# Closing an attention unit ahead of the exponentials, and a rearranged first pair of tiles, in a transformer step on 8 cores

## The reference, cut to what matters

```python
def layer(x, mod):                        # same weights for context and latent tokens
    x += 0.5*gate1 * SwiGLU(RMSNorm(x)*(1+scale1)+shift1)      # FFN 1, 1024 -> 2x2816 -> 1024
    h  = RMSNorm(x)*(1+scale2)+shift2
    dq, dk, dv, gq, gk, gv = split(h @ w_in)                   # 1024 -> 2304
    # 4 differential heads: softmax(q1 k1) - lam*softmax(q2 k2), times v, then RMSNorm of the head
    # 8 grouped query heads on 2 kv heads
    x += gate2 * (concat(o_diff, o_gqa) @ w_out)
    x += 0.5*gate3 * SwiGLU(RMSNorm(x)*(1+scale3)+shift3)      # FFN 2
mod = silu(c) @ w_ada + b_ada             # 9 vectors of 1024: shift, scale, gate, three times
```

## Time and profile before

| | |
|---|---|
| median of 3 runs | 3947.0 us |
| profiled execution | 3947.68 us; span of its slowest core (core 3) 3946.2 us |
| spans of the 8 cores | 3928.2 to 3946.2 us |
| granted TensorE clock, mean | 0.959 to 0.963 |
| busy: PE, DVE, ACT, POOL | 89%, 59%, 52%, 3% |
| DMA | 572.79 MB, 145 GB/s on average |

### The profile page before, as it was taken

How to read it: one execution, slowest core, us unless ns; L and a number is a source line. 1 busy time by engine, 2 the same in 40 slices (tenths; PEclk the granted TensorE clock), 3 DMA queues, 4 the chain that set the end, 5 groups by cost and what they waited for, 6 DMA issues and landing times.

```text
span 3946.2 us, 51478 instructions; the slowest of 8 cores (3928.2 to 3946.2 us)
## 1 busy us (share of the span) xinstructions
PE 3505.6 (89%) x15812; PEld 1523.4 (39%) x15812; DVE 2322.3 (59%) x3013; ACT 2048.4 (52%) x2608; POOL 99.9 (3%) x183
## 2 busy tenths in 40 slices
PE   1996899998869698998999999899989999899988
PEld 0442344443334344444334444333423433334433
DVE  5665774543554755565755676655567655655643
ACT  2213323334443434443576766677776667777631
POOL 0000000001010000000000000000000000000000
PEclk9998899999989799999999999999999999999989
DMA  8787776666536267565523423422233313332232
GB/s 215 174 208 203 210 259 186 197 210 168 166 110 187 77 179 213 176 206 198 165 88 112 136 81 115 152 92 79 90 115 133 106 63 105 133 104 86 89 124 95
DMA packets 134842, 572.79 MB, mean 145 GB/s; under 512 B 16848, under 2 KB 22480, under 8 KB 129744
## 3 DMA queue, kind: packets, MB, share of 16 engines
q1 hardware_dynamic: 118304, 491.56, 37.6%
q0 software_dynamic: 16272, 77.93, 9.2%
HBM read 540.40 MB, written 90.51 MB: 160 GB/s over the span
## 4 chain that ended last, share of the span: by engine, by line
PE 65%; ACT 15%; DVE 9%; issue 6%; DMA 4%; ACTq 0%; DVEq 0%; SPq 0%; POOL 0%; POOLq 0%
PE PSA L464 65%; ACT PT L467 10%; ACT L467 2%; DVE RG L470 1%; DVE MT L473 1%; DVE XB L473 1%; ACT HB L467 1%; DVE FIN L477 1%; DVE FIN L484 1%; DMA DR<-w_dn 1%; DVE PT L473 1%; DMA PT<-w_ada 1%; DVE NS L470 1%; ACT FIN L467 1%; DMA s_vd<-RG 1%
## 5 line engine op out<-in xcount | busy, mean ns | idle before, releaser
L464 PE MATMUL PSA<-HB,WR 128*128 128x512 bf16 x6800 | 1577.4, 388 | 143.1 <-ACT HB L467 58.4
L467 ACT ACTIVATE PT<-PSA 128x1024 bf16<-128x1024 f32 x1184 | 1151.5, 1021 | 344.3 <-PE PSA L464 324.0
L464 PEld LDWEIGHTS PSA<-HB,WR 128*128 128x128 bf16 x6800 | 669.9, 99 | 1025.9 <-issue 290.4
L464 PE MATMUL PSA<-QTS,RG 128*128 128x512 bf16 (+1 forms) x2432 | 659.4, 375 | 74.5 <-ACT PT L467 70.8
L464 PE MATMUL PSA<-PT,RG 128*128 128x512 bf16 (+1 forms) x2368 | 648.4, 381 | 28.8 <-DVE FIN L477 22.8
L464 PE MATMUL PSA<-HID,DR 128*128 128x512 bf16 x2640 | 590.8, 380 | 17.3 <-DMA DR<-w_dn 13.9
L467 ACT ACTIVATE TH<-PSA 128x512 f32<-128x512 f32 x352 | 209.6, 596 | 576.5 <-PE PSA L464 566.9
L473 DVE SCALAR_TENSOR_TENSOR TH<-TH,PSA 128x512 f32<-128x512 f32 x352 | 241.3, 686 | 343.4 <-ACT TH L467 339.6
L464 PEld LDWEIGHTS PSA<-HID,DR 128*128 128x128 bf16 x2640 | 258.0, 98 | 333.5 <-issue 26.1
L464 PEld LDWEIGHTS PSA<-QTS,RG 128*128 128x128 bf16 (+1 forms) x2432 | 195.1, 97 | 467.8 <-issue 333.6
L467 ACT ACTIVATE SQ<-XB 128x512 f32<-128x512 f32 x224 | 139.5, 627 | 431.0 <-DVE XB L473 392.6
(11 more groups left out here) (89 smaller groups left out, 1655.9 us busy)
## 6 DMA issues: line engine op xcount, KB each, us to landing
WR<-s_gu SPq DMA_DIRECT2D x308, 512.0 KB, 4.1
DR<-s_dn SPq DMA_DIRECT2D x112, 704.0 KB, 4.6
RG<-s_kt SPq DMA_DIRECT2D x64, 576.0 KB, 4.1
WR<-s_in SPq DMA_DIRECT2D x65, 512.0 KB, 5.6
RG<-s_vg SPq DMA_DIRECT2D x32, 864.0 KB, 6.4
PT<-w_ada SPq DMA_DIRECT2D x48, 512.0 KB, 8.2
RG<-s_vd SPq DMA_DIRECT2D x32, 576.0 KB, 4.8
XB<-xs SPq DMA_DIRECT2D x8, 2048.0 KB, 9.9
```

The source lines that it names most:

```text
L464: return ("pe", (lambda e: e.matmul(out, lhsT, rhs, start=start, stop=stop)), reads, [PK(bank)], c, None, mode)
L467: return ("act", (lambda e: e.activation(out, in_, func, **kw)), reads, writes, 0.18 + n * 0.00082, None)
```

## The change

Four things are changed. (1) `fin_d` and `fin_g` are spawned with priority 2 and so rank above exponentials, additions and everything else where the planner finds no difference in idle time. (2) For the pair of tiles, the squares are summed by TensorE: `stats_pe` sends each of the eight squares through an fp32 matmul with ones into one bank, and the additions on DVE and the matmul in `norm` fall away. (3) The cast loads of FFN 1 weight blocks 2 and later wait for shift 1 (`MOD 0`) instead of scale 1 (`MOD 1`), and so do the write-backs of blocks 0 to 5; the second tile's x is loaded after 15 pieces of `w_ada` instead of 9. (4) The Silu of c comes right after c's load, and the lambda computation waits until shift 1 is done.

```diff
+            early = kind == "gu0" and idx < NW
+
             def wb():
-                yield [dma("sp", s_w[kind][idx], dst, [key], [("sw", kind, idx)], nsem("wb", 4), nb // 2)]
+                if early:
+                    yield Get(ev(("mod", 0)))
+                yield [dma("sp", s_w[kind][idx], dst, [key] + ([("MOD", 0)] if early else []), [("sw", kind, idx)], nsem("wb", 4), nb // 2)]
                 setf(("wb", kind, idx))
-            gate = [("MOD", 1)] if kind == "gu0" else [("HID", 10)] if kind == "dn0" else []
+            gate = [("MOD", 1) if idx < 2 else ("MOD", 0)] if kind == "gu0" else [("HID", 10)] if kind == "dn0" else []
...
-                    yield Get(ev(("mod", 1)))
+                    yield Get(ev(("mod", 1 if i < 2 else 0)))
...
+        yield [act(CB.rearrange("p g d -> p (g d)"), CB.rearrange("p g d -> p (g d)"), AF.Silu, ["FIN"], ["FIN"], n=2048)]
+        setf("CB")
         yield [dma("sp", BADA[:, :], b_ada[:, :], [], ["BADA"], "c1", 36864)]
...
-        yield [act(CB.rearrange("p g d -> p (g d)"), CB.rearrange("p g d -> p (g d)"), AF.Silu, ["FIN"], ["FIN"], n=2048)]
-        setf("CB")
+        yield Get(ev(("mod", 0)))
...
-                if (m, c) in ((1, 3), (0, 1)):
+                if (m, c) in ((1, 3), (0, 7)):
                     put("xgo")
...
+    def stats_pe(xb):
+
         b = yield Get("bank")
-        yield [mm(PSB[b], ONESF[:, :], NS[:, xb, :], [("NS", xb), "ONESF"], b, cost=0.9)]
+        for c in range(8):
+            s = yield Get("SQ")
+            yield [act(SQ[:, s, :], XB[:, xb, c, :], AF.Square, [("X", xb, c)], [("SQ", s)])]
+            yield [mm(PSB[b], ONESF[:, :], SQ[:, s, :], [("SQ", s), "ONESF"], b, start=(c == 0), stop=(c == 7), cost=0.9)]
+            put("SQ", s)
+        put(("stp", xb), b)
...
-            stats(xb, None, prio)
+            S.spawn(stats_pe(xb), prio)
...
-            yield from norm(xb, 0, 1, h)
+            yield from norm(xb, 0, 1, h, True)
...
-                S.spawn(fin_d(q, u, ot) if kind == "d" else fin_g(q, u, ot), A_PRIO)
+                S.spawn(fin_d(q, u, ot) if kind == "d" else fin_g(q, u, ot), 2)
```

More of the change, by code:

```diff
@@ L645, in stats, with norm @@
         S.spawn(run(), prio)
-    def norm(xb, i, g, h):
-        yield Get(("st", xb))
-        yield Get("NORM")
+    def stats_pe(xb):
         b = yield Get("bank")
-        yield [mm(PSB[b], ONESF[:, :], NS[:, xb, :], [("NS", xb), "ONESF"], b, cost=0.9)]
+        for c in range(8):
[4 more added lines that the diff above has]
+        put(("stp", xb), b)
+    def norm(xb, i, g, h, pe=False):
+        if pe:
+            b = yield Get(("stp", xb))
+            yield Get("NORM")
+        else:
+            yield Get(("st", xb))
+            yield Get("NORM")
+            b = yield Get("bank")
+            yield [mm(PSB[b], ONESF[:, :], NS[:, xb, :], [("NS", xb), "ONESF"], b, cost=0.9)]
         for o in rstd_ops(b, 1.0 / D, RSTD[:, :], ["RSTD"]):
```

## The result

The changed kernel took 3881.63 us (median of 4 runs, 3880.25 to 3888.57), the kernel before 3947.01 in the same session. The ratio is 0.984, with a 95% interval of 0.982 to 0.986: 65 us less, 1.6%. The prediction was 3872 us, with a range from 3840 to 3910.

The account below looks back on a forecast made before the run. The change was taken to pay only where TensorE, the busiest engine, has nothing to do. Attention -42, end -15 and start -19 sum to -76 on 3947.7 us, giving 3872 us, range 3840 to 3910.

Parts of the forecast that it names:

- the end: After the last PV matmuls: HB 8.5 us earlier and a projection of 19 us instead of 25, together -15 us.
- Halts: Attention: fifteen stretches without exponentials, where units wait for closings stuck behind exponentials, vanish, -85 us.
- Pace of keys without filler: Attention: with filler running out earlier, ACT-paced keys lose 17 us less, DVE-paced keys in differential units 4 us more.
- Filled closings: Attention: at 12 of 16 closings, with filler around, ACT has 17.6 us against TensorE's 15.4, +2 each, +24 us.
- Recip and copies without filler: Attention, differential units without filler: grouped closing's copies, reciprocal and product add to DVE's work, 5 us in each of six, +30.
- (b): Attention keys without filler where ACT sets the pace, 0.09 us lost a key; claimed to fall by 17 us.
- more: Rival: the attention's new costs hide behind exponentials running ahead, attention -66, total 3848 us; chance 0.20.
- The start: Before the first HB matmul: shift 1 ready at 63 us instead of 87.6, first HB matmul sooner, -19 us.
- Eaten by the queue: Rival: each closing holds the exponentials 2 us longer, the attention gives only -12, total 3902 us; chance 0.13.
- Switches cost more: Rival: table switches between exponentials in the attention cost another 1.3 us each, total 3903 us; chance 0.05.
- Start gives nothing: Rival: held-back casts leave FFN 1 short of weights and take the 19 us back, total 3891 us; chance 0.07.
- Slower: Rival: a differential closing's chain of about 11 us blocks ACT and holds the exponentials, +100, 4047 us; chance 0.05.

Follow-up runs that it names:

- the start's own run: The changed kernel with both closings put back at the rank of the exponentials, leaving the start's edits alone: 0.9958 of the kernel before, -17 us.

## Why the prediction was right where it was

**The time** is 10 us off the point forecast, within the range, and the forecast case is the one that came: halts gone, filler running out earlier, switches paid for, start and end shorter.

**The step that failed** is in "the end": "HB is there near 3765.5, 8.5 earlier", added to the attention's -42. The attention's window reaches to that very chunk, and the 44 matmuls beside the closing are in its 7478 records. They cost 9.5 us wherever they stand, so the -42 had the gain in it already. The run with only the last closing first shows it: 13.2 of 15.7 us given back. Without the 8.5 the recorded terms give -42 - 6.5 - 19 = -67.5. That they then sum to exactly the span's change is partly luck, as the terms show.

**The attention's terms**, from the loss record by record and the runs:

- Halts, -85: the first 12 keys of differential units lost 119 us before and lose 39 now, -80. That has in it the 15 that grouped closings now add there (below), so the halts gave some 95, ten more than recorded.
- Pace of keys without filler, -17 and +4: the keys 12 to 36 of grouped units lost 37 and, without the 13 of the next item, lose 32, so about -5, not -17; the same keys of differential units lost 27 and lose 39, +12, not +4. The first was too large by some 10, the second too small by 8.
- Filled closings, +24: 13, shown by the kernel without switches. The 17.6 us on ACT against 15.4 named the place and nearly the price, 1.5 to 1.9 us for 2; but such closings are eight, not twelve.
- Recip and copies without filler, +30: those four stretches lose 15 more than the pace of additions; the reciprocal alone is 13 by its own run. The term was twice what came, since four stretches paid, not six, and less than 5 us each.
- Not foreseen: +14 at the beginning of grouped units, where TensorE waits for ACT, most of it in the four ahead of which filler had run out.
- Together: -95 - 5 + 12 + 13 + 15 + 14 = -46, where 189.4 became 144.5. That the recorded terms came to -42 all the same is luck in their errors: the gain of the halts too small, two costs and the gain of (b) too large, the +4 too small, and +14 left out. (These counts end with the last exponential; up to HB it is the -42.5 of the table.)
- The bounds don't follow from the terms: with all new costs hidden these give -103, not -85, and with half as much again and nothing from (b) they give +5.5. The -66 of "more" hides the +24 alone.

**The end**: 24.1 us from the last PV matmuls to the projection's sum, predicted 27. The projection's own part was 16.3, not 19, since TensorE took its 64 matmuls after a pause of 5.68 us at nearly its full pace.

**The start**: -16.2 on the slowest core, predicted -19. (By the recorded terms, squares from 58 and 16.4 us for eight at the low clock give 74.4, not 73.5.) Shift 1 came at 70.1, not 63, the squares at 65.7, not 58, the first HB matmul at 75.6, not 70: the second x was sent at 55.28, not 50, since a piece came late (a wait of 5.77 us for it), and took 10.4 us, not 8. The eight squares took 9.3 us, as in the case of a clock that rises after two: the granted clock is 0.50 from 66 to 69 us and 1.00 from 70 to 75. In the kernel before, the profile has 1.00 for the whole of 38.4 to 89.6, though the fp32 pair took 2.05 us, so there the low clock was read from the duration alone. On the fastest core shift 1 was done at 63.7, and over the cores the median gain at the first exponential was 19 us. The size was right for a middle core, but the slowest one sets the time. Unbroken matmuls came from 90.70, not 85. I had not seen that the gates would be worth next to nothing without TensorE's sums.

**The rivals.** "More" needed the filled closings' costs to hide; the runs show 13 for switches and 13 for the reciprocal, so they did not. "Eaten by the queue" needed 2 us more a closing; filled ones cost less than I had, not more. "Switches cost more" is refuted by the run without them: 0.7 us a load. "Start gives nothing" is refuted by the start's own run. "Slower" needed the whole chain of 11 us to hold ACT; no two exponentials start more than 5.2 us apart, and the waits of 4.1 to 4.2 us in these are for the grouped closing on DVE, not for the differential one's chain. Table loads, 31 in both versions by my count of the order, are 31 from the first exponential on in both traces (28 up to the last exponential and 3 behind it before, 29 and 2 now).

**Still open**: why grouped units without filler begin with 3 us of loss (no run was made for it), and how much of the 15 us that grouped closings bring on top of the differential ones comes from where filler falls rather than from the banks.

## What to carry to other kernels

When work moves out of a gap, ask whether the gap's end comes sooner or the work only stands elsewhere: count what the busiest engine does in the whole window, and never add a term for an event that the window already ends with. When two limits lie on top of each other, as DMA and DVE's order did at the start, parts of a change that are each worth nothing can be worth something together, so undo one part *and* do one part alone before dropping any. And spreading filler evenly is no gain by itself: it pays only where it makes an engine's waits vanish, and thin filler in every unit left nearly as much loss in all (140 us) as full units beside empty ones (144).

## What the runs showed of the hardware

- A table load of 1.28 us between exponentials cost TensorE 0.7 us on average (12.7 us for 18 loads); load and activations around it stood 0.01 to 0.03 us apart.
- A reciprocal of 128x512 fp32 took DVE 3.35 us, a product of the same size 0.69 (2398.49 and 2401.94 on core 5 of the changed kernel). Taking 16 of them out gave 13.0 us in the attention, nearly all of it where no filler stood.
- Of sixteen fp32 matmul records from 66.47 on, after 32.8 us without a matmul, ACT's waits for them went from 1.77 us down to 0.23: the granted clock was 0.50 from 66 to 69 and 1.00 from 70 to 75, so it rose from 1.2 to 2.4 GHz within these few.
- In one execution of the changed kernel the same code had its first HB matmul between 70.1 and 77.8 us after the start, in two groups of four cores (70.1 to 71.8, and 74.5 to 77.8), and in the kernel before between 86.4 and 90.2. So a gain at the start should be read from the slowest cores, and from more than one execution.
